# Paged attention in a hybrid decoder step: each page half gathered in four quarters of its tokens

## The reference, cut to what matters

```python
past = cache_l[page_table].reshape(Bd, -1, KV_CACHE_DIM)          # (8, 4096, 288)
q_lat = jnp.einsum('bthd,chd->bthc', q_nope, lp["w_uk"])
pc, pr = past[..., :KV_LORA_RANK], past[..., KV_LORA_RANK:]
s_past = jnp.einsum('bthc,bkc->bhtk', q_lat, pc) + jnp.einsum('bthr,bkr->bhtk', q_rope, pr)
...
p = jax.nn.softmax(s, axis=-1).astype(new_rows.dtype)
ctx = jnp.einsum('bhtk,bkc->bthc', p[..., :n_past], pc) + jnp.einsum('bhtk,bkc->bthc', p[..., n_past:], nc)
```

## Time and profile before

| | us |
|---|---|
| median of 3 runs | 1026.46 |
| lowest and highest run | 1024.45, 1029.73 |
| the profiled execution's own time | 1024.23 |
| its span, first to last instruction | 1022.4 |
| PE busy | 990.1 (97%) |
| DVE busy | 519.7 (51%) |
| POOL busy | 446.1 (44%), 284 instructions |
| the gathers' queue: packets, data | 2304 packets, 37.75 MB |

### The profile page before, as it was taken

One profiled execution on the slowest core, in us unless ns is written; L12 is line 12 of the kernel. 1 busy time (PEld: TensorE's weight loads), 2 busy tenths in 40 slices (PEclk: granted clock), 3 DMA queues, 4 the chain that ended last, 5 costly groups with the idle time before them and its releaser, 6 DMA issues.

```text
span 1022.4 us, 19821 instructions
## 1 busy us (share of the span) xinstructions
PE 990.1 (97%) x8511; PEld 896.0 (88%) x8511; DVE 519.7 (51%) x731; ACT 298.2 (29%) x598; POOL 446.1 (44%) x284
## 2 busy tenths in 40 slices
PE   6999998998999999999999999999999999999997
PEld 6989898765777777999965899999999999999996
DVE  5789999478555555562255365421342144114323
ACT  7333275465444442220144122200120022002222
POOL 4545687500011102655220255555555555555561
PEclk8999999999999999999999999999999999999999
DMA  8323365504377763622291022322232223322222
GB/s 233 81 67 82 104 195 144 180 22 186 126 276 278 281 269 125 227 83 84 98 402 56 22 86 83 101 83 83 84 100 86 83 84 90 96 83 83 86 80 88
DMA packets 140557, 130.39 MB, mean 128 GB/s; under 512 B 13477, under 2 KB 133170, under 8 KB 136630
## 3 DMA queue, kind: packets, MB, share of 16 engines
q1 hardware_dynamic: 134888, 88.55, 28.6%
q0 software_dynamic: 2304, 37.75, 9.5%
q10 hardware_dynamic: 3278, 2.83, 0.8%
HBM read 123.53 MB, written 5.03 MB: 126 GB/s over the span
## 4 chain that ended last, share of the span: by engine, by line
PE 82%; DVE 12%; ACT 2%; issue 2%; POOL 2%; DMA 1%; SPq 0%; ACTq 0%; DVEq 0%; POOLq 0%
PE gps L582 56%; PE gps L942 5%; PE aux L956 3%; PE aux L983 3%; PE gps L1098 1%; PE gps L1180 1%; PE aux L962 1%; PE gps L1018 1%; PE gps L718 1%; DVE act_lo L1698 1%; PE aux L894 1%; DVE sm L1976 1%; PE aux L1111 1%; PE aux L973 1%; POOL wlo L500 1%
## 5 line engine op out<-in xcount | busy, mean ns | idle before, releaser
L497 POOL TENSOR_SCALAR whi<-wraw 128x1024 fp32r<-128x1024 f32 (+1 forms) x109 | 115.2, 1057 | 358.1 <-PE gps L582 298.6
L582 PE MATMUL gps<-act_hi,whi 128*128 128x272 f32 x912 | 266.2, 292 | 4.9 <-DVE act_lo L1698 4.1
L582 PE MATMUL gps<-act_lo,whi 128*128 128x272 f32 x912 | 264.8, 290 | 0.0
L582 PE MATMUL gps<-act_hi,wlo 128*128 128x272 f32 x912 | 264.3, 290 | 0.0
L500 POOL TENSOR_TENSOR wlo<-wraw,whi 128x1024 fp32r<-128x1024 f32 (+1 forms) x109 | 258.0, 2367 | 9.1
L582 PE MATMUL gps<-h_hi,whi 128*128 128x272 f32 x640 | 185.7, 290 | 0.0
L582 PE MATMUL gps<-h_lo,whi 128*128 128x272 f32 x640 | 185.0, 289 | 0.0
L582 PE MATMUL gps<-h_hi,wlo 128*128 128x272 f32 x640 | 184.6, 288 | 0.0
L582 PEld LDWEIGHTS gps<-act_hi,whi 128*128 128x128 f32 x912 | 172.8, 189 | 5.9 <-issue 3.3
L582 PEld LDWEIGHTS gps<-act_hi,wlo 128*128 128x128 f32 x912 | 172.8, 189 | 0.3 <-issue 0.2
L582 PEld LDWEIGHTS gps<-act_lo,whi 128*128 128x128 f32 x912 | 172.7, 189 | 0.0
(11 more groups left out here) (374 smaller groups left out, 1528.7 us busy)
## 6 DMA issues: line engine op xcount, KB each, us to landing
wraw<-in_w_up_dram SPq DMA_DIRECT2D x32, 512.0 KB, 4.0
wraw<-in_w_down_dram SPq DMA_DIRECT2D x32, 512.0 KB, 3.7
wraw<-in_w_in_dram SPq DMA_DIRECT2D x14, 512.0 KB, 4.1
kv<-in_cache_mem_k_dram SPq DMA_DIRECT2D x7, 1024.0 KB, 6.9
kv<-in_cache_mem_v_dram SPq DMA_DIRECT2D x7, 1024.0 KB, 13.9
wraw<-in_w_mem_k_dram SPq DMA_DIRECT2D x16, 256.0 KB, 3.0
wraw<-in_w_mem_v_dram SPq DMA_DIRECT2D x16, 256.0 KB, 3.0
wraw<-in_w_out_dram SPq DMA_DIRECT2D x8, 512.0 KB, 4.5
```

Of the source, the lines that this page charges most:

```text
L497: nc.gpsimd.tensor_scalar(whi[:, slot, 0:n], wraw[:, slot, 0:n], 1.0, 1.0, ALU.mult, ALU.mult).then_inc(pool_step, 1)
L582: mm = nc.tensor.matmul(out_of(a), w_of(w, k), x_of(x, k, part), start=(k == 0 and s == 0), stop=(k == k_tiles - 1 and s == 2))
```

## The change

`idx` gets four columns of row numbers for each turn, and one more for what it held before. The cache is seen as rows of 4 tokens (4,608 bytes), 32 to a page. The old row number goes to `idx[:, 4, :]`; quarter i has four times that plus i. `gather(n)` issues four indirect DMAs, each of which fills 4 of the 16 tokens in every partition. Each raises the same semaphore by 16, so that both waits for a page half are for 64 where they were for 16. All that lies behind `idx` in the core's memory moves up by 256 bytes in each partition.

```diff
-        idx = keep("idx", [128, 16], U32)
+        idx = keep("idx", [128, 5, 16], U32)
...
-        rows_of_pages = cache_mla[0].rearrange("a (e k) n -> (a e) (k n)", e=8)
+        rows_of_pages = cache_mla[0].rearrange("a (e k) n -> (a e) (k n)", e=32)
...
             def gather(n):
-                nc.gpsimd.indirect_dma_start(
-                    pg[n % 4][:, :, :].rearrange("p k d -> p (k d)"), None, rows_of_pages,
-                    bass.IndirectOffsetOnAxis(ap=idx[:, n:n + 1], axis=0)).then_inc(page_in[n % 4], 16)
+                for i in range(4):
+                    nc.gpsimd.indirect_dma_start(
+                        pg[n % 4][:, 4 * i:4 * i + 4, :].rearrange("p k d -> p (k d)"), None, rows_of_pages,
+                        bass.IndirectOffsetOnAxis(ap=idx[:, i, n:n + 1], axis=0)).then_inc(page_in[n % 4], 16)
...
-                pe.wait_ge(page_in[n % 4], 16 * (n // 4) + 16)
+                pe.wait_ge(page_in[n % 4], 64 * (n // 4) + 64)
...
-            V.tensor_scalar(idx[:, :], ptw[:, :], 8.0, lane[:, 0:1], ALU.mult, ALU.add).then_inc(idx_ok, 1)
+            step(V.tensor_scalar(idx[:, 4, :], ptw[:, :], 8.0, lane[:, 0:1], ALU.mult, ALU.add))
+            for i in range(4):
+                ins = V.tensor_scalar(idx[:, i, :], idx[:, 4, :], 4.0, float(i), ALU.mult, ALU.add)
+            ins.then_inc(idx_ok, 1)
...
-                dve.wait_ge(page_in[n % 4], 16 * (n // 4) + 16)
+                dve.wait_ge(page_in[n % 4], 64 * (n // 4) + 64)
```

## The result

The changed kernel took 1038.49 us (median of 8 runs, 1033.13 to 1041.34) beside 1026.12 us for the kernel before (8 runs, 1024.45 to 1029.73): ratio 1.0107, interval 1.0094 to 1.0121. The forecast was 1027.0 us and "the same", with 1031 as the upper end. It is slower, and by more than any case but rival B allowed. Ratios leave out three executions of batch five that ran far slower than all others: one of the changed kernel (2477 us) and two of the kernel before (1214 and 2477 us).

A forecast was written before the change was run, and what follows sets the result against it. PE was taken to bound the kernel (82% of the chain of waits), gathers hardly in it. All terms were 0 but +0.5 us for index work: 1024.2 + 0.5 = 1024.7 profiled, 1027.0 for the median; range 1023.5 to 1031.

The forecast's parts named there:

- rival B: Loop of 12 gathers: quarters do not overlap on POOL's queue; 16 us later, 1043, or 86 us, 1112; chance 0.07.
- The issues, and whether they hold others: POOL, four issues for one: 2.8 us added per turn, all in POOL's idle time ahead of gathers; cost 0.
- step (2): Landing of a page half: quarters issued every 0.94 us, last lands at 9.5 us, 6.4 us of margin; cost 0.
- Gathers beside DVE in the prompt attention: Twelve more issues beside DVE there, neither holding the other: cost 0; 5.6 us if each held DVE half its length.
- The index work: Four more DVE instructions and a dependent step before the prompt attention: +0.5 us (0.3 to 1.5), carried to the end.
- rival A: Around the index work and scans, DVE and POOL take turns in another order: +1.6 us, 1028.1; chance 0.22.
- rival C: PE's granted clock in the prompt attention moves: 1.8 us gained or lost, 1025.2 or 1028.8; chance 0.08.
- the waits for 64: Both page waits: same number of wait instructions on the same semaphores, satisfied when the last quarter lands; cost 0.
- the shift: Buffers behind the index table move by 256 bytes, none against another; cost 0.
- D: A gain, as smaller pieces let other queues in sooner; the loop has 0.2 us to give, 1026.3; chance 0.03.
- the 0.04 kept for what no one had seen: Chance 0.04 left for unseen effects anywhere in the kernel, half each way, with no size given.
- signs of failure: Wrong if PE waits for pages, an indirect DMA takes over 2 us, or prompt-attention DVE instructions stretch beside gathers.

The follow-up runs named there:

- batch five: Last batch, on one chip: the changed kernel again (1029.39 us) and it with pauses between the quarters of all sixteen gathers (1029.40 us); kernel before 1026.79 us.
- e11: Kernel before plus three 32-byte-a-partition gathers, which nothing reads, behind each whole gather; second measurement, batch three: 1035.81 us in one run.
- f2: Kernel before plus twelve waited-for memsets of 128x128 on POOL behind each of gathers 4 to 15, no added DMA: 1026.24 us in one run.
- f4: Changed kernel with two memsets as a pause ahead of the second, third and fourth quarter of gathers 4 to 15: 1029.65 us, 1.0040.
- e12: Changed kernel with the four gathers of a page half issued later in the turn, behind the signal for pTs: 1062.69 us in one run.
- f3: Changed kernel with six memsets as a pause between the second and third quarter of gathers 4 to 15: 1034.38 us, 1.0077.
- e3: Changed kernel with gathers 0 to 3 whole, quarters only in gathers 4 to 15: 1032.40 us, 1.0049.
- e1: Changed kernel with all five index columns computed but each page half fetched by one whole gather: 1028.51 us, 1.0020.
- e4: Changed kernel with quarters only for gathers 0 to 3, gathers 4 to 15 whole: 1029.26 us, 1.0023.
- e8: Kernel before plus three 32-byte-a-partition gathers, which nothing reads, behind each whole gather; first measurement, batch two: 1026.13 us in one run.
- e5: The changed kernel again, unaltered, as yardstick of batch two: 1027.53 us, 1.0021.
- f6: The changed kernel again, unaltered, as yardstick of the last batch: 1029.39 us, 1.0024.
- e7: Changed kernel with each quarter issued only when the last but one has landed, two in flight at most, on two semaphores: 1053.24 us, 1.0256.
- e9: The changed kernel again, unaltered, as yardstick of batch three: 1037.22 us, 1.0119.
- e10: Changed kernel with three gathers, of 8, 4 and 4 tokens, for a page half; second measurement, batch three: 1032.99 us in one run.
- e2: Changed kernel with two gathers of eight tokens for a page half and three index columns: 1027.55 us, 1.0015.

## Why the prediction was wrong

**The issues, and whether they hold others: the step that failed.** The prediction hid them in POOL's 7.60 us of idle time ("All of it is idle time, cost 0"). That was right for POOL: four issues of 0.94 us, started 1.24 us apart and not the 0.94 us of its step (2), and 4.3 us of idle time left. It took an issue to cost only the engine that executes it. In three of the changed kernel's five measurements PE's signals are held from the third or fourth issue until about a microsecond behind it, and PE's signals release DVE. In a turn without slack on PE, DVE's copies come late, PE's next matmuls with them, and a turn gets 0.4 to 0.5 us longer. e11 (issues without data) shows that it is the issue; f2 (work without issues) that it isn't POOL's being busy; f4 (the same issues 1.70 us apart) that it is their spacing, on one chip; e12 and f3 that it follows them through the turn. The rows of before had only single gathers, with 7.60 us of idle time between them, so nothing in them priced a row of issues; the step should have been bounded from above, not set at 0. In sum the loop carries +6.6 of the 8.9 us in the profiled execution, and 3.9 us by e3 against e1.

**Gathers beside DVE in the prompt attention: "Neither holds the other."** DVE's instructions were not stretched, as forecast. But on held chips PE's signals beside gathers 1 and 2 were up to 2.6 us late. What that costs is small: e4 is 0.8 us over e1, within the error.

**The index work: half its size, and wrong in form.** The term was +0.5 (0.3 to 1.5), carried one for one to the end. DVE in the changed kernel, then POOL:

```profile
101.08 1.57 DVE L1844 TENSOR_SCALAR idx<-ptw,lane 128x16 uint32<-128x16 int32 x1
102.68 0.41 DVE L1846 TENSOR_SCALAR idx<-idx 128x16 uint32<-128x16 uint32 x4
...
104.89 1.49 DVE L1797 TENSOR_TENSOR lrv<-lrv,xc 128x544 f32<-128x544 f32 x1
106.42 3.30 DVE L1798 TENSOR_TENSOR_SCAN xc<-lra,lrv 128x512 f32<-128x512 f32 x1
...
123.01 0.66 DVE L1748 TENSOR_TENSOR gate<-gps,rs 128x544 f32<-128x544 f32 x1
```

```profile
104.44 1.38 POOL L497 TENSOR_SCALAR whi<-wraw 128x1024 fp32r<-128x1024 f32 x1 [1.82 <-PE gps L583]
105.89 2.74 POOL L500 TENSOR_TENSOR wlo<-wraw,whi 128x1024 fp32r<-128x1024 f32 x1
```

The gate's last scaling comes at 123.01 (before 122.21, forecast 122.7). As the first index instruction starts 0.25 us earlier here (101.08, before 101.33), the work between the two is 1.05 us longer, twice the forecast. The four new instructions with the step take 0.4 us of it, as forecast: from the start of the first index instruction to the first product 1.92 us instead of 1.49 (103.00 - 101.08, 102.82 - 101.33). The other 0.6 us is rival A's exchange of turns (below). No more than 0.3 us is left at the first gather (198.2 against 197.9). So the delay fades. What stays is a cost of rival C's kind, the clock: PE waits 2.8 instead of 1.7 us for the gate, and in 11 of the 16 profiles of kernels with this index work a stretch of 3.4 to 6.8 us at half clock follows at 123 to 127 us; in the four without it (before, e8, e11, f2) there is none. By e1, e5 and f6 the index work with all that follows it is worth 1.6 to 2.6 us in the median; what part of that is the clock's wasn't separated. The result's own trace has no such stretch at 123 us; its half clock is in the prompt attention, 6.8 us from 252.4 on where the kernel before has 3.4. The upper end of 1031 had room for this, not for both.

**The landing, the waits for 64, and the shift: right.** In e5, which has all landing records, the last quarter lands 9.6 to 11.1 us behind the first issue, 10.2 in the median where the forecast was 9.5, within the margin, and PE never waits for a page. The four quarters thus don't follow one another at a full price each. The Trainium skill, "DMA: Bandwidth & Descriptors", section Anatomy of one DMA, gives about 2.0 us for each DMA plus the bytes at 436 GB/s, which is, as an estimate, 13.4 us for four quarters one after the other. The 10.2 us don't bear that out. The Trainium skill, in the same section, puts most of the fixed part down to the wait for the write's receipt; that this part overlaps between quarters is the prediction's own inference, and the 10.2 us fit it.

**The rivals.** A came by its mechanism, at less than its price. POOL's L497 at 104.44 went ahead of DVE's second product, which took 1.49 us in place of 0.70 and ended at 106.38; POOL's L500 (to 108.63) then held the second scan, which took 3.30 us in place of 1.94 and ended at 109.72 (A had 109.3 + 1.23 = 110.5). But the third product, which POOL had held before (2.23 us), now took 0.71. DVE was through with the scans at 114.09, not 114.9 (before 113.28). B's arithmetic was shown by e7, but the changed kernel's quarters overlap as forecast. C's kind of loss came in some profile of every batch, mostly at 123 us, where the rival had not looked, and in the result at its own place. D didn't. The case that decided was the 0.04 kept for what no one had seen. For a change that issues 48 more DMAs of a kind seen only singly, a range that ended 4 us above the forecast was too narrow, and its signs of failure (PE waiting for pages, an indirect DMA over 2 us, DVE's instructions "stretched beside gathers") looked at durations, where the cost sat in signals.

**What stays open.** Why two chips of five are free of it (or free in that hour); by what way POOL's issues hold PE's signals alone; why e12's lateness is larger; whether pauses free gathers 1 and 2.

Every execution was recorded by the profiler, and its part in it wasn't tried: a kernel run without it could differ, and this rival stands. The traces give it weight: the held ones lack records. The changed kernel leaves 7413 records of rising semaphores on each free chip, and 7106, 7122 and 7162 where it is held; three gathers leave 7156 free and 7137 held, and the tiny ones 7405 and 7355. In e9 a quarter of the landing records is missing (771 of 1024); in e10 all 768 of the gathers are there, and the 19 that are missing are others. In f4 landing records are missing (877 of 1024) also in the loop, where no signal is late, so missing records don't by themselves mean late signals.

The Trainium skill, "NOTIFIC — the notification-queue block", section 7.1, says that the block which writes an engine's records holds the engine back rather than lose one inside; PE has the most records by far (8511 matmuls and as many weight loads of 19873 instructions), so this is a candidate, and no run here shows it.

Of the 12.4 us between the medians the profiled executions show 8.9; the other 3.5 weren't traced, the profile being the fastest of the eight.

No version with split gathers beat the kernel before. Halves (e2) come closest, at 1.0015 [0.9997, 1.0034].

## What to carry to other kernels

Splitting a gather gains nothing when its landing was never waited for, and added issues can cost beyond the issuing engine: space POOL's indirect DMAs (1.70 us apart held nothing in the loop here, 1.24 did), or issue at most two in a turn (e2); two, a pause of 1.8 us and two more weren't free (f3). When an engine seems late though its input is finished, compare the time of the semaphore with the end of the instruction that raises it, see whether records are missing, and run the same kernel on several chips before settling on a cause. An operation the trace of before shows only singly has no price in a row of four; put the unknown in the range.

## What the hardware showed that was not expected

- Three or four indirect DMAs on POOL at 1.24 us apart hold PE's semaphore signals until 0.8 to 1.07 us behind the end of the third or fourth; 0.9 and 1.9 us late in the changed kernel, 3.8 us in e12. Signals of DVE, ACT and POOL were never late. On two of the five chips of the batches it didn't happen at all. On held chips single issues (f2: 0.18 us at most), two in a row and no more in a turn (e2: 0.37 us at most) and issues 1.70 us apart (f4, in the loop) hold next to nothing. All this is seen in executions that the profiler recorded.
- An indirect DMA's issue costs POOL 0.94 us whatever it brings: a whole page half, a quarter, or 32 bytes a partition (e11).
- With at most two in flight a quarter takes 4.4 to 6.0 us from issue to landing (e7), a whole half by itself 8.4 to 10.3. A quarter of the bytes took half of the time or more.
- PE's wait of 2.7 to 2.8 us for the gate, at about 122 us, was followed by half clock (0.50) for 3.4 to 6.8 us in 11 of 16 profiles; after the wait of 1.7 us it was in none of four.
